# Meta tokens brought in turned by 16 element-wise transfers, output quarters 3 turned off TensorE, and the decay gates' steps moved one unit forward, in a three-layer fp32 kernel

## The chip, the cores and the metric

One NeuronCore of a Trainium2 chip runs the whole program. The metric is the device time of one execution in microseconds, the median of several runs. Lower is better.

## What is computed

A 256 x 2048 activation `x` goes through three layers, all in fp32. Cut to what matters here:

```
# layer 1: 16 heads, stick-breaking attention
q, k, v, g = split(rms_norm(x) @ w_in_a, 4);  o = attention(q, k, v)
x = x + rms_norm((o * silu(g)) @ w_out_a);    x = x + (p0 @ w_pp0) * sigmoid(x @ w_pg0)
# layer 2: 16 heads, latent attention
cq, g = split(rms_norm(x) @ w_in_b);          o = mla(rms_norm(cq) @ w_uq, k, v)
x = x + rms_norm((o * silu(g)) @ w_out_b);    x = x + (p1 @ w_pp1) * sigmoid(x @ w_pg1)
# layer 3: 16 meta tokens (16 x 2048) are put ahead of the 256 rows
h = concat([meta_tokens, x])
q, k, v, r, glr, pu = split(rmsnorm(h) @ w_in)
logg = log_sigmoid(glr @ gate_w2 + gate_b) / 16      # the decay gates
... gated linear attention in chunks of 64 (sums of logg), pooling, w_out, MLP, final norm
```

Every weight is read once from HBM. Each fp32 product is made of three products of rounded parts (high x high, high x low, low x high).

## The kernel before, in words

**Weights.** All weight matrices come in units of 128 partitions x 1024 fp32 (512 KB), numbered through the whole program by `plan()`. SyncE (SP) loads them in order into a ring of four `raw` slots (`load`, L405), one as soon as VectorE (DVE) has made the low part of the unit four before it (`lo_done`). ScalarE (ACT) makes the high part `whi` (L1155) once TensorE (PE) has used the unit four before; DVE makes the low part `wlo` (L1751); PE multiplies. A unit is 12 matmuls of 128 x 512 in most stages (L538 to L540 in `unit`) and 24 matmuls of 272 columns in the stages `k2`, `v2`, `pu` (L978 to L980 in `columns`). A chunk of a stage is eight units (four in `k2` and the like). ACT's and DVE's loops (`along`) take, for step uu of a chunk, first the split of the unit three ahead and then the "hooks" written for that step; PE's loops run the hooks of a step ahead of its matmuls. So the order of the work on each engine is written out by hand.

**Turned operands.** PE needs activations with the channel on the partitions. There are two ways. In the first, PE transposes a batch of four 128 x 128 blocks into PSUM (`batch`, L550; `turn` and `turns` call it for a tensor's eighth f), and ACT (`hi_batch`, L1193) and DVE (`lo_batch`, L1788) split it. In the second, for quarters listed in `MOVED`, nothing runs on PE: DVE transposes 32 x 32 blocks straight into place in `mov` (`blocks_turned`, L1810, four instructions a band of 32 partitions). For quarters also listed in `FLIPPED`, DVE first makes two big block transposes into `stg` (`flipped`, L1799), then ACT copies two of the four bands (`bands_moved`, L1207, four each) and DVE makes the other two itself. Then ACT splits the high part (`hi_moved`, L1216, L1220) and DVE the low part (`lo_moved`, L1823, L1827). PE's wait for a quarter is in `operands`. `mov` holds one quarter at a time, so one quarter's band copies wait for the low part of the quarter before.

The gated attention output, `ogA` in layer 1 and `ogB` in layer 2, is the operand of the stages `out_a` and `out_b`. Before: `ogA` quarter 2 (eighths 4 and 5) goes by DVE; quarter 3 (eighths 6 and 7) and all of `ogB` go through PE. PE makes eighths 6 and 7 at unit 4 of the first chunk of `out_a` and `out_b` (`OG_LATE`) and needs them at unit 6. DVE writes the last quarter of the gated output (`gated`, L1985) just ahead of that chunk.

**Meta tokens.** One DMA (L468) brings them as 16 rows into `metax`. At unit 6 of the last chunk of `gate1` PE turns them (`turn_meta`, 16 transposes of 16 x 128 into one PSUM bank, L550). DVE multiplies them by the norm gain (L1999) into `scaledM`; ACT takes the squares of `metax` (L1367, four), then copies the high part `lhi` (L1370); DVE makes the low part `llo` (L2002). PE waits for that low part between the last chunk of `gate1` and the stage `q2`.

**Decay gates.** In the first chunk of `k2` PE makes the gate logits ahead of unit 2 (`gate_logits`, L915 and L916). Before them come: `glrT` (DVE L2243, step 0), the high part `glrS` (ACT L1561, step 1), `gw2lo` (DVE L2248, step 1) and the low part of `glrS` (DVE L2251, step 1). Then ACT takes |.|, exp and log (L1568, L1573, L1578) in steps 2 and 3 and in step 0 of the second chunk, DVE the gates (L2259, step 1 of the second chunk), and PE sums them ahead of the second chunk's unit 3 (`sums_from_start`, L923).

Of the kernel before, what the change touches and what calls it, by code (L numbers as in the profile page):

```python
# [21 lines left out]
P = 128  # L22
# [29 lines left out]

LAST = {4: [6, 7]}
BLK = 32
FLIPPED = [("x1", 3), ("x3", 3), ("x5", 3)]
MOVED = [(name, c) for name, cs in (("ogA", [2]), ("x1", [3]), ("x2", [0, 1, 2]), ("x3", [3]), ("x4", [0, 1, 2]), ("x5", [0, 1, 2, 3])) for c in cs]
X1_LATE = {1: [4, 5]}
OG_EARLY, OG_LATE = {6: [0, 1]}, {"ogA": {0: [2, 3], 4: [6, 7]}, "ogB": {0: [2, 3], 2: [4, 5], 4: [6, 7]}}
MIXED_EARLY = {7: [0, 1]}

UNIT = 1024
# [41 lines left out]
def join(*hooks):  # L103

    return {u: [f for h in hooks for f in h.get(u, [])] for u in sorted({u for h in hooks for u in h})}
# [40 lines left out]
def build(nc, w, const, out):  # L146
# [3 lines left out]
    with ctx:  # L150
# [142 lines left out]
        def sem(name):  # L293
            if name not in sems:
                sems[name] = ctx.enter_context(nc.semaphore(name))
            return sems[name]
# [8 lines left out]


        NORMS = ("pre0", "post0", "pre1", "kvl", "ql", "post1", "norm1", "norm2")
        order = [("gcol", 1), ("x0", 8), ("p", 2), ("norms", 1), ("ogA", [0, 1, 2, 3, 6, 7]), ("x1", 6), ("x2", [6, 7]), ("ckv", 2), ("kr", 1),
                 ("cq", 2), ("ogB", [0, 1, 2, 3, 4, 5, 6, 7]), ("x3", 6), ("meta", 1),
                 ("x4", [6, 7]), ("rsb", 1), ("qdec", 2), ("kend", 2),  # L310
                 ("vT", 4), ("kvM", 1), ("mixed", 4)]
        whole = ("gcol", "norms", "kr", "rsb", "qdec", "kend", "vT", "kvM")
# [35 lines left out]
        def gate_chunk_at(j):  # L348

            return S["attb"].c0 + min(2 * j + 2, SLOTS - 1) + j  # L350
# [47 lines left out]
        def _(sp):  # L398
# [8 lines left out]
            def stage(name, lo=0, hi=None):  # L407
                s = S[name]
                for j in range(lo, s.chunks if hi is None else hi):
                    for uu in range(s.units):  # L410
                        load(s, j, uu)
# [49 lines left out]
            stage("out_b", 0, 1)  # L461
            sp.wait_ge(sem("attB_o"), HEADS // 2)
            sp.dma_start(gains[:, :], w["norm_post"][1:2, :].to_broadcast((P, D))).then_inc(sem("post_in1"), 16)
            stage("out_b", 1)
            stage("ple1")
            stage("gate1", 0, 1)
            sp.wait_ge(evac_dve, S["out_b"].c0 + 4)
            sp.dma_start(metax[0:META, :], w["meta_tokens_2"]).then_inc(sem("meta_in"), 16)  # L468
            latents = w["w_in_2"][0, :, V0 + 2 * GLA_H * DV:V0 + 2 * GLA_H * DV + GRANK].rearrange("(k p) n -> p k n", p=P)
            for j in (1, 2):  # L470
                stage("gate1", j, j + 1)
                half = slice((j - 1) * (KT // 2), j * (KT // 2))
                sp.dma_start(graw[:, half, :], latents[:, half, :]).then_inc(sem("latents_in"), 16)
            stage("gate1", 3)
# [24 lines left out]
        def _(pe):  # L499
# [236 lines left out]
                    hooks = join(hooks, {6: [lambda: pe.wait_ge(sem("attA_o"), HEADS // 2)]}, turns("ogA", OG_EARLY))  # L736
                product(S["g"], j, mhi, mlo, hooks=hooks)

            def turn_meta():
                pe.wait_ge(sem("meta_in"), 16)  # L740
                batch([(metax[0:META, k * P:(k + 1) * P], META, k * META) for k in range(KT)])

            def post(layer, y, x1, x2):

                ab = "ab"[layer]
                def gates_out():
                    pe.wait_ge(evac_act, gate_chunk_at(3) + 1)
                late = turns(y, OG_LATE[y])
                for hook in late.pop(0):
                    hook()  # L750
                for j in range(4):
                    product(S[f"out_{ab}"], j, bhi, blo, need=y if j == 0 else None, free=gates_out if layer and j == 0 else None, hooks=late if j == 0 else {})
                for j in range(4):
                    product(S[f"ple{layer}"], j, phi[:, layer], plo[:, layer])
                    if j % 2:
                        for f in (j - 1, j):
                            turn(x1, f)
                for j in range(4):
                    hooks = {} if j else turns(x1, X1_LATE)
                    if layer and j == 3:  # L760
                        hooks = join(hooks, {6: [turn_meta]})
                    product(S[f"gate{layer}"], j, *((ahi, alo) if layer else (bhi, blo)), need=x1 if j == 0 else None, hooks=hooks)

            post(0, "ogA", "x1", "x2")
# [126 lines left out]
                    mm = pe.matmul(tp[n % 2][:, META + t * P:META + (t + 1) * P], ones, diag[:, t, :], start=True, stop=True)  # L891
                mm.then_inc(tp_full, 1)

            pe.wait_ge(tp_done, BATCH["meta", 0][0] + 1)
            def latents():

                pe.wait_ge(tp_done, BATCH["x4", 7][0] + 1)
# [83 lines left out]
                    mm.then_inc(unit_used, 1)  # L981
            product(S["q2"], 0, x4hi, x4lo, need="x4", hooks=join(turns("x4", LAST), {7: [turn_rs]}))
            latents()
            columns("k2", 0, {2: [gate_logits]})
            columns("k2", 1, {3: [sums_from_start]})
            columns("v2", 0, {2: [sums_to_end]})
            columns("v2", 1, {1: [lambda f=f: turn_decayed_queries(f) for f in range(2)], 3: [lambda t=t: turn_keys(t) for t in range(TT)]})
# [150 lines left out]
        def _(act):  # L1138
# [221 lines left out]
            def meta_in():  # L1360

                act.wait_ge(sem("meta_in"), 16)
                for i in range(4):
                    n = sq[0]
                    sq[0] += 1
                    act.wait_ge(sem("squares"), n - 1)
                    act.activation(xb[n % 2][0:META, 0:CH], metax[0:META, i * CH:(i + 1) * CH], ACT.Square,  # L1367
                                   accum_out=ssqM[0:META, i:i + 1]).then_inc(sem("squares"), 1)
                act.wait_ge(sem("meta_scaled"), 1)
                act.activation(lhi[:, :, 0:META], scaledM[:, :, :], ACT.Copy).then_inc(tp_hi, 1)  # L1370
                act.wait_ge(sem("latents_in"), 32)
                act.activation(gwT[:, :, 0:GRANK], graw[:, :, :], ACT.Copy).then_inc(sem("latents_hi"), 1)

# [224 lines left out]
            def columns(name, j, dst, hooks={}):  # L1598
# [2 lines left out]
                along(s, j, hooks)  # L1601
                ended(s, j)
                act.activation(dst, acc[(s.c0 + j) % 2][0][:, 0:LEN], ACT.Copy).then_inc(evac_act, 1)
            columns("k2", 0, kT[:, 0, :], {0: [gate_hi], 1: [latents_hi], 2: [gate_abs], 3: [gate_exp]})
            columns("k2", 1, kT[:, 2, :], {0: [gate_log], 3: [exps_from_start]})
            for j, hooks in enumerate(({2: [exps_to_end]}, {}, {}, {})):
                columns("v2", j, vT[:, 2 * j, :], hooks)

# [129 lines left out]
        def _(dve):  # L1738
# [249 lines left out]
            for j in range(4):  # L1988
                along(s, j, ahead=softplus_of(3 + j), hooks=join(attention_of(3 + j), join(los("ogA", bhi, blo, None, OG_EARLY),
                                                                             {2 * q + 1: [lambda q=q: blocks_turned("ogA", 2, q)] for q in range(P // BLK)}) if j == 3 else {}))  # L1990
                gated(s.c0 + j, (s.c0 + j) % 2, j, sem("attA_o"), 2 * (j + 1))

            rsM = rs[0:META, 7, 0:1]

            def meta_in():

                n, k = BATCH["meta", 0]
                dve.wait_ge(tp_full, n + 1)
                dve.tensor_tensor(scaledM[:, :, :], tp[n % 2][:, 0:KT * META].rearrange("p (k m) -> p k m", m=META),  # L1999
                                  gcol[:, GC["norm1"]:GC["norm1"] + KT][:, :, None].to_broadcast((P, KT, META)), ALU.mult).then_inc(sem("meta_scaled"), 1)  # L2000
                dve.wait_ge(tp_hi, k + 1)
                dve.tensor_tensor(llo[:, :, 0:META], scaledM[:, :, :], lhi[:, :, 0:META].bitcast(F32), ALU.subtract).then_inc(tp_done, 1)  # L2002
                dve.wait_ge(sem("latents_hi"), 1)
                dve.tensor_tensor(gwT[:, :, GRANK:], graw[:, :, :], gwT[:, :, 0:GRANK].bitcast(F32), ALU.subtract).then_inc(sem("latents_lo"), 1)
                sq[0] += 4
                dve.wait_ge(sem("squares"), sq[0] + 6)
                dve.tensor_reduce(ssumM[0:META, :], ssqM[0:META, :], AX, ALU.add).then_inc(sem("metan_ssum"), 1)
# [192 lines left out]
            for c in range(SLOTS):  # L2200
                more = c + 1 < SLOTS
                scores_out(c)
                for k, (query, uu) in enumerate(slot_units(c)):
                    split_to(u + 4)
                    u += 1
                    if query and uu == 1:
                        dve.wait_ge(unit_used, u)
                        queries_out(c + 1, (*acc[0], tp[0]))
                    if more and k == 3:
                        roped_queries(c + 1)  # L2210
                    if more and k == 4:
# [90 lines left out]

            def values_turned(h):
                turned_out("vT", h, vC[:, :, h * DV:(h + 1) * DV])
            columns("k2", 0, kT[:, 0, :], kT[:, 1, :], sem("kT"), {0: [latents_out], 1: [latents_split]})
            columns("k2", 1, kT[:, 2, :], kT[:, 3, :], sem("kT"), {1: [log_gates]})
            for j, hooks in enumerate(({1: [keys_from_start], 3: [keys_to_end]},
                                       {1: [lambda f=f: decayed_queries_out(f) for f in range(2)],
                                        3: [lambda t=t: turned_out("kend", t, kend[:, t, :]) for t in range(TT)]},
# [234 lines left out]
```

## Time and profile before

| | |
|---|---|
| median of 3 runs (lowest to highest) | 2059.88 us (2059.24 to 2059.95) |
| the profiled execution's own time | 2059.53 us |
| its span in the profile | 2057.7 us |
| PE busy | 2046.2 us (99%) |
| DVE busy | 1315.2 us (64%) |
| ACT busy | 1103.1 us (54%) |
| DMA traffic | 375.49 MB, q1 at 60.0% of 16 engines |

A busy time is the time in which an engine had a compute instruction in flight. PE's matmuls are pipelined: the start of one to the start of the next (0.23 us for 512 columns) is what one costs, while its own duration is shown as 0.39 us. So what a group of instructions costs PE is read from starts. The profiled time is 0.35 us under the median, and 1.8 us of it lie outside the span.

### The profile page before, as it was taken

What the parts mean: (1) busy time and instruction counts of PE and PEld (TensorE: products, weight loads), DVE (VectorE), ACT (ScalarE), POOL (GpSimd) and SP (SyncE); (2) the same over time, 40 slices, a digit from 0 to 9 for tenths busy, and PEclk for the clock granted to TensorE, in tenths of its full rate; (3) what the DMA queues carried; (4) which work ended last, traced back from release to release, by engine and by line L of the source; (5) the groups of instructions that cost most, each with busy time, mean ns of one, the idle gap of its engine ahead of it and who ended that gap; (6) DMA issues with size and microseconds to landing.
All of it is one profiled execution on the core that took longest, in us unless ns stands there. A gap on an engine that the chain in (4) does not pass through costs nothing.

```text
span 2057.7 us, 27144 instructions
## 1 busy us (share of the span) xinstructions
PE 2046.2 (99%) x10712; PEld 1755.5 (85%) x10712; DVE 1315.2 (64%) x1722; ACT 1103.1 (54%) x1581; POOL 6.1 (0%) x12
## 2 busy tenths in 40 slices
PE   9999999999999999999999999999999999999998
PEld 8888888888898888888889988888888888888886
DVE  6555556757877777658955567976556556555554
ACT  6444566646566787546664355565335434434444
POOL 0000000000000000000000000000000000000000
PEclk9999999999999999999999999999999999999999
DMA  8666655665656555565645446666666666666664
GB/s 278 186 186 192 174 154 155 188 191 173 201 173 191 169 143 164 182 194 184 195 148 155 137 140 224 194 192 186 195 195 185 194 195 185 193 193 189 191 195 144
DMA packets 211165, 375.49 MB, mean 182 GB/s; under 512 B 13875, under 2 KB 48917, under 8 KB 210518
## 3 DMA queue, kind: packets, MB, share of 16 engines
q1 hardware_dynamic: 211046, 373.85, 60.0%
q8 instruction: 81, 1.33, 0.3%
q14 instruction: 38, 0.31, 0.1%
HBM read 371.71 MB, written 2.10 MB: 182 GB/s over the span
## 4 chain that ended last, share of the span: by engine, by line
PE 98%; ACT 1%; DVE 0%; DMA 0%; issue 0%; SPq 0%; ACTq 0%; DVEq 0%
PE acc L538 19%; PE acc L540 19%; PE acc L539 19%; PE acc L1094 6%; PE acc L644 3%; PE tp L1094 3%; PE xb L1094 3%; PE acc L1097 3%; PE acc L978 2%; PE acc L980 2%; PE acc L979 2%; PE tp L644 1%; PE xb L644 1%; PE acc L647 1%; PE xb L1097 1%; PE tp L1097 1%
## 5 line engine op out<-in xcount | busy, mean ns | idle before, releaser
L1751 DVE TENSOR_TENSOR wlo<-raw,whi 128x1024 fp32r<-128x1024 f32 x633 | 771.9, 1224 | 591.8 <-ACT whi L1155 589.8
L1155 ACT ACTIVATE whi<-raw 128x1024 fp32r<-128x1024 f32 x633 | 668.3, 1059 | 741.0 <-PE acc L540 430.5
L538 PE MATMUL acc<-whi,both 128*128 128x512 f32 (+1 forms) x976 | 375.8, 385 | 0.0
L540 PE MATMUL acc<-whi,both 128*128 128x512 f32 (+1 forms) x976 | 374.0, 383 | 0.0
L539 PE MATMUL acc<-wlo,both 128*128 128x512 f32 (+1 forms) x976 | 373.8, 383 | 0.0
L540 PEld LDWEIGHTS acc<-whi,both 128*128 128x128 f32 x976 | 183.2, 188 | 36.1
L538 PEld LDWEIGHTS acc<-whi,both 128*128 128x128 f32 x976 | 183.3, 188 | 34.7
L539 PEld LDWEIGHTS acc<-wlo,both 128*128 128x128 f32 x976 | 183.3, 188 | 34.0
L1094 PE MATMUL acc<-bT,whi 128*128 128x512 f32 x512 | 160.7, 395 | 0.0
L538 PE MATMUL acc<-whi,bhi 128*128 128x512 f32 x384 | 150.0, 391 | 0.0
L540 PE MATMUL acc<-whi,blo 128*128 128x512 f32 x384 | 149.5, 389 | 0.0
L539 PE MATMUL acc<-wlo,bhi 128*128 128x512 f32 x384 | 149.4, 389 | 0.0
L1097 PEld LDWEIGHTS acc<-bT,wlo 128*128 128x128 f32 x512 | 96.2, 188 | 22.7
L538 PE MATMUL acc<-whi,aT 128*128 128x512 f32 x256 | 101.4, 396 | 0.0
L1097 PE MATMUL acc<-bT,wlo 128*128 128x256 f32 x512 | 100.6, 278 | 0.0
L540 PE MATMUL acc<-whi,aT 128*128 128x512 f32 x256 | 99.9, 390 | 0.0
L539 PE MATMUL acc<-wlo,aT 128*128 128x512 f32 x256 | 99.7, 389 | 0.0
L978 PE MATMUL acc<-lhi,whi 128*128 128x272 f32 x320 | 93.4, 292 | 0.0
L980 PE MATMUL acc<-lhi,wlo 128*128 128x272 f32 x320 | 92.2, 288 | 0.0
L979 PE MATMUL acc<-llo,whi 128*128 128x272 f32 x320 | 91.5, 286 | 0.0
L540 PEld LDWEIGHTS acc<-whi,blo 128*128 128x128 f32 x384 | 72.1, 188 | 15.1
L539 PEld LDWEIGHTS acc<-wlo,bhi 128*128 128x128 f32 x384 | 72.1, 188 | 14.8
(417 smaller groups left out, 3191.2 us busy)
## 6 DMA issues: line engine op xcount, KB each, us to landing
raw<-in_mlp_w SPq DMA_DIRECT2D x256, 512.0 KB, 4.3
raw<-in_w_in_a SPq DMA_DIRECT2D x128, 512.0 KB, 3.8
raw<-in_w_ple_gate SPq DMA_DIRECT2D x64, 512.0 KB, 4.3
raw<-in_w_in SPq DMA_DIRECT2D x64, 512.0 KB, 3.8
raw<-in_w_in_b SPq DMA_DIRECT2D x40, 512.0 KB, 3.9
raw<-in_w_out_a SPq DMA_DIRECT2D x32, 512.0 KB, 4.2
raw<-in_w_out_b SPq DMA_DIRECT2D x32, 512.0 KB, 4.3
raw<-in_w_out SPq DMA_DIRECT2D x32, 512.0 KB, 4.5
```

What stands on the lines that cost most here:

```text
L538: pe.matmul(o, hi[:, kt, tok], whi[:, slot, wc], start=start, stop=False)
L539: pe.matmul(o, hi[:, kt, tok], wlo[:, slot, wc], start=False, stop=False)
L540: mm = pe.matmul(o, lo[:, kt, tok], whi[:, slot, wc], start=False, stop=stop)
L644: pe.matmul(tiles[q % 2][ct][:, :], whi[:, slot, wc[ct]], aT[:, kt, :, :].rearrange("p i t -> p (i t)"), start=first and k == 0, stop=False)
L647: mm = pe.matmul(tiles[q % 2][ct][:, 0:SEQ], wlo[:, slot, wc[ct]], aT[:, kt, 0, :], start=False, stop=end)
L978: pe.matmul(o, whi[:, slot, wc], lhi[:, kt, :], start=first and k == 0, stop=False)
L979: pe.matmul(o, whi[:, slot, wc], llo[:, kt, :], start=False, stop=False)
L980: mm = pe.matmul(o, wlo[:, slot, wc], lhi[:, kt, :], start=False, stop=last and k == s.kt - 1)
L1094: pe.matmul(banks[ct][:, :], whi[:, slot, wc[ct]], bT[:, kt, :, :].rearrange("p i t -> p (i t)"), start=first and k == 0, stop=False)
L1097: mm = pe.matmul(banks[ct][:, 0:SEQ], wlo[:, slot, wc[ct]], x5hi[:, kt, :], start=False, stop=end)
L1155: act.activation(whi[:, u % RING, 0:n], raw[:, u % RING, 0:n], ACT.Copy).then_inc(hi_done, 1)
L1751: dve.tensor_tensor(wlo[:, u % RING, 0:n], raw[:, u % RING, 0:n], whi[:, u % RING, 0:n].bitcast(F32), ALU.subtract).then_inc(lo_done, 1)
```

## The change

Three edits. (1) `ogA` and `ogB` quarter 3 join `FLIPPED` and `MOVED` (so do the eighths 6 and 7 leave `OG_LATE`): DVE flips the quarter right behind the last `gated`, ACT and DVE move its bands, split it in step 4 of the first chunk. (2) Meta tokens are loaded a second time, turned, by 16 DMAs of 128 x 16 single elements into `scaledM`, one behind every third weight unit from the second chunk of `out_b` to the third of `gate1`; `turn_meta` leaves PE, and DVE multiplies `scaledM` in place. The plain load of `metax` stays, for the squares. (3) In `k2` the gates' steps move: ACT's high part to step 0, |.| to 1, exp to 2, log to 3; DVE's split to step 0 and its gates to step 0 of the second chunk; PE's logits to unit 1. PE's sums stay where they are.

```diff
-FLIPPED = [("x1", 3), ("x3", 3), ("x5", 3)]
-MOVED = [... ("ogA", [2]), ("x1", [3]), ("x2", [0, 1, 2]), ("x3", [3]), ...]
+FLIPPED = [("ogA", 3), ("x1", 3), ("ogB", 3), ("x3", 3), ("x5", 3)]
+MOVED = [... ("ogA", [2, 3]), ("x1", [3]), ("x2", [0, 1, 2]), ("ogB", [3]), ("x3", [3]), ...]
-OG_EARLY, OG_LATE = {6: [0, 1]}, {"ogA": {0: [2, 3], 4: [6, 7]}, "ogB": {0: [2, 3], 2: [4, 5], 4: [6, 7]}}
+OG_EARLY, OG_LATE = {6: [0, 1]}, {"ogA": {0: [2, 3]}, "ogB": {0: [2, 3], 2: [4, 5]}}
 # SP
-            stage("out_b", 1)
-            stage("ple1")
-            stage("gate1", 0, 1)
+            def with_meta(name, lo, hi, first):
+                s = S[name]
+                for j in range(lo, hi):
+                    for uu in range(s.units):
+                        load(s, j, uu)
+                        m = first + (j - lo) * s.units + uu
+                        if m % 3 == 2 and m // 3 < KT:
+                            k = m // 3
+                            sp.dma_start(scaledM[:, k, :], w["meta_tokens_2"][:, k * P:(k + 1) * P].rearrange("m p -> p m"), allow_slow_non_contiguous=True).then_inc(sem("meta_turned"), 16)
+            with_meta("out_b", 1, NCH, 0)
+            with_meta("ple1", 0, NCH, 24)
+            with_meta("gate1", 0, 1, 28)
...
-                stage("gate1", j, j + 1)
+                with_meta("gate1", j, j + 1, 28 + 8 * j)
 # PE
-                    if layer and j == 3:
-                        hooks = join(hooks, {6: [turn_meta]})
-            pe.wait_ge(tp_done, BATCH["meta", 0][0] + 1)
+            pe.wait_ge(sem("meta_lo"), 1)
-            columns("k2", 0, {2: [gate_logits]})
+            columns("k2", 0, {1: [gate_logits]})
 # ACT
-            columns("k2", 0, kT[:, 0, :], {0: [gate_hi], 1: [latents_hi], 2: [gate_abs], 3: [gate_exp]})
-            columns("k2", 1, kT[:, 2, :], {0: [gate_log], 3: [exps_from_start]})
+            columns("k2", 0, kT[:, 0, :], {0: [gate_hi, latents_hi], 1: [gate_abs], 2: [gate_exp], 3: [gate_log]})
+            columns("k2", 1, kT[:, 2, :], {3: [exps_from_start]})
 # DVE, behind the last gated() of layer 1 (and the same for layer 2)
+            dve.wait_ge(evac_dve, s.c0 + 4)
+            flipped(nat, 3, 1)
-                dve.wait_ge(tp_full, n + 1)
-                dve.tensor_tensor(scaledM[:, :, :], tp[n % 2][:, 0:KT * META]..., gcol[...], ALU.mult)
+                dve.wait_ge(sem("meta_turned"), 16 * KT)
+                dve.tensor_tensor(scaledM[:, :, :], scaledM[:, :, :], gcol[...], ALU.mult)
-            columns("k2", 0, kT[:, 0, :], kT[:, 1, :], sem("kT"), {0: [latents_out], 1: [latents_split]})
-            columns("k2", 1, kT[:, 2, :], kT[:, 3, :], sem("kT"), {1: [log_gates]})
+            columns("k2", 0, kT[:, 0, :], kT[:, 1, :], sem("kT"), {0: [latents_out, latents_split]})
+            columns("k2", 1, kT[:, 2, :], kT[:, 3, :], sem("kT"), {0: [log_gates]})
```

## Rows read from the trace of the kernel before

**Rows 1.** The page: the chain that ended last, share of the span by engine.
```profile
PE 98%; ACT 1%; DVE 0%; DMA 0%; issue 0%; SPq 0%; ACTq 0%; DVEq 0%
```

**Rows 2.** Waits of PE: who waited for whom, us in total, times, longest.
```profile
PE tp L915 <- DVE glrS L2251: 0.7, 1, 0.7
```

**Rows 3.** Timeline of PE, first chunk of out_a: start us, us, instruction.
```profile
408.89 0.39 PE L540 MATMUL acc<-whi,blo 128*128 128x512 f32 x1
...
410.23 0.40 PE L539 MATMUL acc<-wlo,bhi 128*128 128x512 f32 x1
...
415.45 0.39 PE L538 MATMUL acc<-whi,bhi 128*128 128x512 f32 x1
```

**Rows 4.** Timeline of DVE around the start of out_a.
```profile
399.03 1.23 DVE L1985 TENSOR_TENSOR nat<-nat,stg 128x1024 f32<-128x1024 f32 x1
400.17 1.22 DVE L1751 TENSOR_TENSOR wlo<-raw,whi 128x1024 fp32r<-128x1024 f32 x1
401.31 1.28 DVE L1788 TENSOR_TENSOR blo<-tp,bhi 128x512 fp32r<-128x512 f32 x2
...
403.64 1.22 DVE L1823 TENSOR_TENSOR blo<-mov,bhi 128x1024 fp32r<-128x1024 f32 x1
```

**Rows 5.** Timeline of DVE at the start of out_b, then PE at its unit 4.
```profile
838.22 1.23 DVE L1985 TENSOR_TENSOR nat<-nat,stg 128x1024 f32<-128x1024 f32 x1
...
849.71 1.03 PE L550 MATMUL tp<-tab,nat 128*128 128x128 f32 x8
```

**Rows 6.** Timeline of DVE, then ACT, where x1's flipped quarter is moved.
```profile
501.58 1.30 DVE L1799 STREAM_TRANSPOSE stg<-x 128x512 f32<-128x512 f32 x2
...
508.19 1.79 DVE L1810 STREAM_TRANSPOSE mov<-x 32x256 f32<-32x256 f32 x4
...
502.91 1.70 ACT L1207 ACTIVATE mov<-stg 32x256 f32<-32x256 f32 x4 [1.29 <-DVE stg L1799]
```

**Rows 7.** Timeline of PE: end of gate1, start of q2.
```profile
1021.76 0.39 PE L540 MATMUL acc<-whi,both 128*128 128x512 f32 x1
...
1023.51 0.40 PE L539 MATMUL acc<-wlo,both 128*128 128x512 f32 x1
...
1028.75 0.40 PE L538 MATMUL acc<-whi,lhi 128*128 128x512 f32 x1
...
1037.05 0.40 PE L538 MATMUL acc<-whi,lhi 128*128 128x512 f32 x1
```

**Rows 8.** Timeline of ACT, then DVE, in the same stretch.
```profile
1027.27 0.40 ACT L1370 ACTIVATE lhi<-scaledM 128x256 fp32r<-128x256 f32 x1
...
1027.70 0.42 DVE L2002 TENSOR_TENSOR llo<-scaledM,lhi 128x256 fp32r<-128x256 f32 x1 [0.72 <-ACT lhi L1370]
...
1035.36 4.62 DVE L1751 TENSOR_TENSOR wlo<-raw,whi 128x1024 fp32r<-128x1024 f32 x4
```

**Rows 9.** Timeline of PE, then DVE, at the gates in k2.
```profile
1062.48 0.29 PE L980 MATMUL acc<-lhi,wlo 128*128 128x272 f32 x1
1063.50 0.48 PE L915 MATMUL tp<-gw2hi,glrS 65*128 65x512 f32 x1 [0.73 <-DVE glrS L2251]
...
1079.85 0.29 PE L980 MATMUL acc<-lhi,wlo 128*128 128x272 f32 x1
1080.54 2.05 PE L923 MATMUL tp<-tab,logg 128*128 128x128 f32 x16 [0.40 <-DVE loggM L2259]
...
1062.81 0.43 DVE L2251 TENSOR_TENSOR glrS<-glrT,glrS 32x272 fp32r<-32x272 f32 x1
```

**Rows 10.** DMA in 970.0 to 970.5 us: packets, then queue, MB, share.
```profile
DMA packets 575, 0.08 MB, mean 164 GB/s; under 512 B 552, under 2 KB 552, under 8 KB 575
...
q1 hardware_dynamic: 575, 0.08, 111.6%
```

**Rows 11.** DMA in 969.0 to 969.5 us: the queue, packets, MB, share.
```profile
q1 hardware_dynamic: 60, 0.12, 75.3%
```

**Rows 12.** Second chunk of gate1: engines' busy us; last, PE clock, DMA share, GB/s.
```profile
962.00:984.00 22.00, 22.00 (x99) 18.23 (x98) 20.12 (x31) 12.34 (x19) 0.00 (x0) 1.00 0.65 207
```

More of the change, by code:

```diff
@@ L54 @@
 BLK = 32
-FLIPPED = [("x1", 3), ("x3", 3), ("x5", 3)]
-MOVED = [(name, c) for name, cs in (("ogA", [2]), ("x1", [3]), ("x2", [0, 1, 2]), ("x3", [3]), ("x4", [0, 1, 2]), ("x5", [0, 1, 2, 3])) for c in cs]
+FLIPPED = [("ogA", 3), ("x1", 3), ("ogB", 3), ("x3", 3), ("x5", 3)]
+MOVED = [(name, c) for name, cs in (("ogA", [2, 3]), ("x1", [3]), ("x2", [0, 1, 2]), ("ogB", [3]), ("x3", [3]), ("x4", [0, 1, 2]), ("x5", [0, 1, 2, 3])) for c in cs]
 X1_LATE = {1: [4, 5]}
-OG_EARLY, OG_LATE = {6: [0, 1]}, {"ogA": {0: [2, 3], 4: [6, 7]}, "ogB": {0: [2, 3], 2: [4, 5], 4: [6, 7]}}
+OG_EARLY, OG_LATE = {6: [0, 1]}, {"ogA": {0: [2, 3]}, "ogB": {0: [2, 3], 2: [4, 5]}}
 MIXED_EARLY = {7: [0, 1]}
@@ L307, in build @@
         NORMS = ("pre0", "post0", "pre1", "kvl", "ql", "post1", "norm1", "norm2")
-        order = [("gcol", 1), ("x0", 8), ("p", 2), ("norms", 1), ("ogA", [0, 1, 2, 3, 6, 7]), ("x1", 6), ("x2", [6, 7]), ("ckv", 2), ("kr", 1),
-                 ("cq", 2), ("ogB", [0, 1, 2, 3, 4, 5, 6, 7]), ("x3", 6), ("meta", 1),
+        order = [("gcol", 1), ("x0", 8), ("p", 2), ("norms", 1), ("ogA", [0, 1, 2, 3]), ("x1", 6), ("x2", [6, 7]), ("ckv", 2), ("kr", 1),
+                 ("cq", 2), ("ogB", [0, 1, 2, 3, 4, 5]), ("x3", 6),
                  ("x4", [6, 7]), ("rsb", 1), ("qdec", 2), ("kend", 2),
@@ L737, in _ @@
                 product(S["g"], j, mhi, mlo, hooks=hooks)
-            def turn_meta():
-                pe.wait_ge(sem("meta_in"), 16)
-                batch([(metax[0:META, k * P:(k + 1) * P], META, k * META) for k in range(KT)])
             def post(layer, y, x1, x2):
@@ L1369, in meta_in @@
                 act.wait_ge(sem("meta_scaled"), 1)
-                act.activation(lhi[:, :, 0:META], scaledM[:, :, :], ACT.Copy).then_inc(tp_hi, 1)
+                act.activation(lhi[:, :, 0:META], scaledM[:, :, :], ACT.Copy).then_inc(sem("meta_hi"), 1)
                 act.wait_ge(sem("latents_in"), 32)
@@ L1991, in _ @@
                 gated(s.c0 + j, (s.c0 + j) % 2, j, sem("attA_o"), 2 * (j + 1))
+            dve.wait_ge(evac_dve, s.c0 + 4)
+            flipped(nat, 3, 1)
             rsM = rs[0:META, 7, 0:1]
             def meta_in():
-                n, k = BATCH["meta", 0]
-                dve.wait_ge(tp_full, n + 1)
-                dve.tensor_tensor(scaledM[:, :, :], tp[n % 2][:, 0:KT * META].rearrange("p (k m) -> p k m", m=META),
+                dve.wait_ge(sem("meta_turned"), 16 * KT)
+                dve.tensor_tensor(scaledM[:, :, :], scaledM[:, :, :],
                                   gcol[:, GC["norm1"]:GC["norm1"] + KT][:, :, None].to_broadcast((P, KT, META)), ALU.mult).then_inc(sem("meta_scaled"), 1)
-                dve.wait_ge(tp_hi, k + 1)
-                dve.tensor_tensor(llo[:, :, 0:META], scaledM[:, :, :], lhi[:, :, 0:META].bitcast(F32), ALU.subtract).then_inc(tp_done, 1)
+                dve.wait_ge(sem("meta_hi"), 1)
+                dve.tensor_tensor(llo[:, :, 0:META], scaledM[:, :, :], lhi[:, :, 0:META].bitcast(F32), ALU.subtract).then_inc(sem("meta_lo"), 1)
                 dve.wait_ge(sem("latents_hi"), 1)
@@ L2218, in _ @@
                     gated(gate_chunk_at(c // 2), 0, c // 2, sem("attB_o"), c + 1)
+            dve.wait_ge(evac_dve, gate_chunk_at(3) + 1)
+            flipped(nat, 3, 1)
             post(1, "ogB", "x3", "x4", GC["norm1"], "norm1")
```

## The prediction

> **What bounds the kernel now.** I read the chain that ended last first: 98% of the span is PE's own work [rows 1]. So the time is the sum of PE's instructions plus PE's few waits. Second, the list of PE's waits. It has five rows, the longest 1.1 us at the very start; the largest that the change touches is the gate logits' wait for DVE [rows 2], and the sums' wait of 0.40 us is in the timeline [rows 9]. No weight unit is waited for, so raw DMA arrival bounds nothing yet. Third, the timelines of PE, DVE and ACT at the four places that the change touches: an item taken from PE pays in full only if the item that PE then meets is ready. Last, the DMA, since the change adds transfers to SP's only queue: its engines were busy 65% of a chunk of `gate1` [rows 12].
>
> What a piece of work costs PE is the gap between the starts around it less the steady pitch of 0.2277 us.
>
> **Part 1: output quarters off PE.** Removed at unit 4 of `out_a`: eight transposes. From L540 at 408.89 to L539 at 410.23 are 1.34 us, two pitches are 0.455, so they cost 0.885 us [rows 3]. `out_b` has the same pattern. Gross 1.77 us.
> What comes instead must be ready when PE enters unit 6. For `out_a` that is 415.45 - 0.885 = 414.57. DVE, in order: the gating ends at 399.03 + 1.23 = 400.26 [rows 4]; the flip waits for it, then takes 1.30 [rows 6], to about 401.6. Then L1751 at a pitch of 1.14 (400.17 to 401.31) and the two L1788 at about 1.19 [rows 4]: 402.7, 403.9. Step 1: L1751, L1823 at 1.14 each: 406.2. Step 2: L1751 and four band transposes (1.82 with their start) [rows 6]: 409.2. Step 3, the same: 412.1. Step 4: L1751, 413.3, then the low split, to be begun at 413.4 and done, at 1.22, at 414.6. ACT does not set this: its first bands wait for the low split of quarter 2 at 406.3, take 1.70 each [rows 6], and with two weight splits between them end at about 410.8, before DVE's. Its high split needs DVE's last band (412.2) and is done by 413.3.
> From the end of a DVE result to PE's start were 0.05 us for `loggM` and 0.26 for `glrS` (62.81 + 0.43 to 63.50) [rows 9]. So PE can start unit 6 between 414.65 and 414.86, against 414.57: a new wait of 0.1 to 0.3 us, I take 0.2. Net for `ogA`: 0.69. Queued behind DVE's flip are only weight splits three units ahead, which have 8 us.
> For `out_b` there is no quarter 2 in the way. The gating ends at 839.45 [rows 5], the flip at 840.8, steps 0 to 3 hold four L1751, two pairs of L1788 and two sets of bands (4.56 + 2.38 + 3.64): 851.4; the last L1751 and the low split: 853.8. PE enters unit 6 at 849.71 + 2 x 2.73 = 855.17 [rows 5]. Spare 1.3 us, so the full 0.885 comes. Eighths 4 and 5 slip by 1.3 us and still come 1.3 ahead of unit 4. Bounds: `ogA` 0 to 0.885, `ogB` 0.5 to 0.885. Part 1: **1.57 us**.
>
> **Part 2: meta tokens.** Removed from PE at unit 6: L540 at 1021.76 to L539 at 1023.51 are 1.75, less 0.455: 1.30 us [rows 7]. But PE then waits ahead of `q2` for `llo`, which was done at 1027.70 + 0.42 = 1028.12 [rows 8]. The chain behind it (ACT: weight split, high split of x4, four squares, `lhi`; then DVE) starts at PE's end of unit 5 and holds nothing that the change takes away; the PSUM read that DVE is spared had already landed. PE would arrive at 1028.75 - 1.30 = 1027.45 and go on at 1028.17 to 1028.38: gain 0.37 to 0.58. A second gate stands behind: `wlo` of `q2`'s unit 3 is the first of four at 1035.36, done by 1036.6 [rows 8], PE used it at 1037.05 [rows 7], and it hangs on ACT's same chain. That lets 0.2 to 0.4 through. I take **0.3 us** of 1.30; bounds 0 and 0.4.
>
> **Part 3: the 16 transfers.** Each moves 128 x 16 single elements: 2048 pieces, 128 for each of 16 DMA engines. The trace has no 4-byte pieces. The nearest row is the load of the gate columns, pieces of 64 B: in half a microsecond 111.6% of 16 engines, 8.9 us, went to 552 small and 23 large pieces [rows 10]; large ones take 0.753 x 0.5 x 16 / 60 = 0.100 us [rows 11]; so (8.9 - 2.3) / 552 = 12 ns a piece. Upper bound: a 4-byte piece as dear as a large one, 100 ns; lower bound: nothing. I take 12 ns, the nearest row: 128 x 12 = 1.5 us of all engines for each transfer. They stand behind every third unit, over 48 units or 131 us, of which 35% are free [rows 12], 46 us; 16 x 1.5 = 25 us fit. A single one delays a weight unit by 1.5 us; a unit is asked for some 8 us ahead of ACT's use and landed in about 4.3 (page), and ACT and DVE are up to three units (8 us) ahead of PE. SP's issue took 0.47 us for the gate columns, and SP mostly waits. Cost **0**. If the cover goes: per piece t ns, 16 x 0.128 t us less 46 us less some 12 us of lead; the point is near 28 ns, and each 10 ns beyond cost 20 us. At 100 ns it is 147 us.
> The Trainium skill speaks against this edit ("DMA: Bandwidth & Descriptors", section "Rules for kernel authors"): a last dimension that isn't contiguous becomes one descriptor for each element, and a plain DMA with a rearranged pattern is 19 times slower than the hardware transpose. Estimate from that page: if the 128 KB went at 19 times the cost at the weights' rate here (some 300 GB/s when busy, 0.43 us), they would take 8 us in all, and still be hidden; by the row of 64-byte pieces it is 25 us. Either leaves the sum as it is.
>
> **Part 4: gates a step ahead.** The logits: L980 at 1062.48 to L915 at 1063.50 is 1.02, the pitch there 0.125 us, so 0.89 lost [rows 9]. The last input, the low part of `glrS`, now hangs on `glrT` (done 1057.2) plus ACT 0.42 and DVE 0.43 with a 0.68 us split beside: ready by 1058.5. PE meets it a unit (3.0 us) sooner than before, at 1059.6: no wait, 0.89 won. The sums: 1079.85 to 1080.54 is 0.69, less 0.125: 0.57 lost [rows 9]. The log now ends in the first chunk's step 3, at about 1072.3; DVE's gates follow the chunk's evacuation and one weight split, 1074.8 to 1076.8. PE comes at about 1079.1: no wait, 0.57 won. ACT's and DVE's weight splits behind the moved steps are 1 to 3 us later than PE frees them, against three units of lead. Part 4: **1.45 us**; bounds 0.9 and 1.5.
>
> **Sum.** 1.57 + 0.3 + 0 + 1.45 = 3.3 us, from the profiled 2059.53 to 2056.2; the median of the runs lies 0.35 higher, so 2059.88 - 3.3 = **2056.6 us**. About 0.2% (4.1 us) is what a measurement can tell from no change: faster means under 2055.8, slower over 2064.0. So the forecast is "no change that can be told", by a small real gain.
>
> **Rivals.**
> (a) Slower: the element-wise DMAs cost more than 28 ns a piece. All 2048 pieces of one transfer read 4 B out of 16 short stretches of 512 B, which 64-byte pieces did not do; this speaks for it. Against: 64-byte pieces already were far below the large ones and took 12 ns. At 36 ns a piece (three times the row): 16 x 4.6 - 58 = 16 us, 2056.6 + 16 = 2073. Decides from 28 ns on. Chance 0.16.
> (b) Faster by over 0.2%: every removed piece pays in full: 1.77 + 1.30 + 1.45 = 4.5 us, 2055.4. For it: PE is 98% of the chain. Against: the chain behind `llo` ends 0.7 us after PE would come. It decides from 4.1 us on; also without the meta part's full gain, if cold starts saved elsewhere add 0.8. Chance 0.13.
> (c) Less comes: DVE, 20.1 us busy of 22 in `gate1` [rows 12], is late behind delayed weights or flips, and `ogA`'s wait is 0.9, not 0.2. Gain 1.5 to 2, 2058.1. Chance 0.18.
> (d) The change doesn't do what it says, the gates' wait only moves: PE at unit 1 waits for ACT's `glrS`. Gain 1.9, 2058.0. Against: ACT sat idle 4.8 us there. Chance 0.03.
> Forecast: 0.50.
>
> **How the numbers follow.** Forecast, (c) and (d) are within 0.2%, 0.71; with the ends of (b) that fall short, and the small overruns of (a) that are under 4 us, taken as they stand: faster 0.13, same 0.70, slower 0.17. Range: down to 2055.4, all of (b)'s price; up past (c) to 2061.5, a start of (a), which leaves out most of (a)'s 0.16. The likeliest case's own range is 2056.0 to 2057.6.
>
> **What would show it.** L550's groups at unit 4 of `out_a` and `out_b` and the 16 x 16 one in `gate1` gone. PE's waits: none at L915 and L923; new ones of 0.1 to 0.3 us at `out_a`'s unit 6 for `blo` (L1823's place) and of about 0.8 us at `q2`'s first matmul for `llo`. The DMA share in `out_b` and `gate1` up from 0.65 to about 0.8, with 32768 more small pieces, and no ACT split waiting long for `raw`. I am wrong if PE's waits name `wlo` in `out_b` to `gate1` (then (a)), if the wait ahead of `q2` is missing (then (b)), or if `out_a`'s unit 6 starts on time.

## Result and profile after

The changed kernel takes 2124.87 us, median of 4 runs (2122.51 to 2126.32), against 2059.56 us for the kernel before: ratio 1.0315, 95% interval [1.0303, 1.0327]. It is 65 us slower where 3.3 us less were forecast. Its profiled execution is the one of 2126.32 us, span 2124.5 us.

Two lines of its page follow: the engines' busy time, and the chain that ended last, where [rows 1] had PE at 98%.

```profile
PE 2068.4 (97%) x10680; PEld 1765.9 (83%) x10680; DVE 1324.1 (62%) x1740; ACT 1110.0 (52%) x1595; POOL 6.1 (0%) x12
```

```profile
PE 87%; DMA 9%; DVE 2%; SPq 1%; ACT 0%; issue 0%; ACTq 0%
```

DMA now holds 9% of the chain. PE's waits (us in total, times, longest), of which [rows 2] has gone:

```profile
PE acc L547 <- DVE wlo L1754: 38.0, 13, 5.8
PE acc L547 <- ACT pp L1415: 2.6, 1, 2.6
PE acc L547 <- DVE llo L2006: 2.3, 1, 2.3
PE tp L559 <- DVE both L1791: 2.1, 1, 2.1
```

`wlo` in `out_b` to `gate1` is what the prediction named as the sign that it is wrong. DVE is not the cause: it waits for ACT's `whi`, and the waits of ACT say what ACT stood for:

```profile
ACT whi L1158 <- DMA raw<-in_w_out_b: 54.1, 17, 10.5
ACT whi L1158 <- DMA raw<-in_w_ple_gate: 50.6, 17, 10.6
```

In the kernel before, ACT waited for neither. So the weights come late. The list of DMA issues (number, KB, us to landing) has `out_b`'s weight units at 10.3 us, while `out_a`'s, with no turned transfer among them, stayed at 4.3, and a turned one of 8 KB at 15.9:

```profile
raw<-in_w_out_a SPq DMA_DIRECT2D x32, 512.0 KB, 4.3
raw<-in_w_out_b SPq DMA_DIRECT2D x32, 512.0 KB, 10.3
...
scaledM<-in_meta_tokens SPq DMA_DIRECT2D x16, 8.0 KB, 15.9
```

SP's timeline in `out_b` (start, us, instruction) shows the period: one turned transfer, three units, and the next one 12.1 to 13.7 us later, where PE takes 8.2 us for three units. Most of the time in `load` (L405) is SP waiting for a free buffer.

```profile
862.31 0.77 SPq L472 DMA_DIRECT2D scaledM<-in_meta_tokens  x1
863.12 12.89 SPq L405 DMA_DIRECT2D raw<-in_w_out_b  x3
876.05 0.47 SPq L472 DMA_DIRECT2D scaledM<-in_meta_tokens  x1
876.56 11.59 SPq L405 DMA_DIRECT2D raw<-in_w_out_b  x3
888.19 1.92 SPq L472 DMA_DIRECT2D scaledM<-in_meta_tokens  x1
```

The lists of the 16 turned transfers, of this kernel and of the one cut by token (below), which is free of the fault, give their first and last issue; the third line is the landing here:

```profile
L472 SPq DMA_DIRECT2D scaledM<-in_meta_tokens x16: 472/710/1922, 850.1 to 1038.2; - x16
...
L472 SPq DMA_DIRECT2D scaledM<-in_meta_tokens x16: 465/472/1025, 849.6 to 976.4; - x16
...
DMA to landing us min/median/max: 14.2/15.9/17.4
```

The 15 periods take 188.1 us against 126.8, 12.5 each against 8.5: 61 of the 70 us between the two spans. The DMA of a single microsecond within such a stretch (869 to 870: packets, then queue, packets, MB, share of 16 engines) shows what a turned transfer does:

```profile
DMA packets 279, 0.01 MB, mean 11 GB/s; under 512 B 274, under 2 KB 274, under 8 KB 279
...
q1 hardware_dynamic: 279, 0.01, 15.6%
```

274 small pieces and 5 large ones go in it, and the engines count as busy 16% of the time. In [rows 10] 552 small pieces went in half that time beside 23 large ones. The pieces are few and their engines idle: they are held by something that the busy share does not show. That is why the DMA share, which I wanted at about 0.8, fell; windows of a stretch of `out_b`, then of `gate1` (columns as in [rows 12]):

```profile
861.00:900.00 39.00, 30.71 (x122) 24.23 (x121) 12.24 (x12) 11.68 (x17) 0.00 (x0) 0.91 0.45 122
...
1020.00:1040.00 20.00, 14.22 (x55) 11.29 (x53) 9.43 (x16) 4.28 (x7) 0.00 (x0) 0.83 0.36 94
```

The granted clock is under 1 as well. After a wait of 4.76 us PE goes on at a pitch of 0.43 us instead of 0.2277, and the clock granted from 882.6 to 886 is 0.50, the lower of the two levels (1.2 of 2.4 GHz):

```profile
882.67 0.79 PE L547 MATMUL acc<-whi,bhi 128*128 128x512 f32 x1 [4.76 <-DVE wlo L1754]
883.27 0.63 PE L548 MATMUL acc<-wlo,bhi 128*128 128x512 f32 x1
883.69 0.63 PE L549 MATMUL acc<-whi,blo 128*128 128x512 f32 x1
...
887.96 0.51 PE L547 MATMUL acc<-whi,bhi 128*128 128x512 f32 x1
888.31 0.40 PE L548 MATMUL acc<-wlo,bhi 128*128 128x512 f32 x1
```

Against the version by token (PE busy 2043.9 us, PE's waits 2.6 us, span 2054.5) the 70.0 us are 45.4 us more of PE waiting (48.0 in all) and 24.5 us more of PE busy with as many instructions. This splits PE's time; it does not make the slower matmuls a second cause. The DMA's own time already gives the period: 7.7 us for a turned transfer (first look, below) and 4.9 us for three weight units (60% of 8.2 us, the DMA share before) are 12.6 us, and 12.5 were measured. In `out_b` each turned transfer is issued, 10.8 to 13.7 us after the one before it, when that one has not landed (14.2 us at least). And the period with the slow matmuls above in it (876.05 to 888.19) took 12.1 us, the one before it, at full clock, 13.7. So the slow matmuls seem to fill time in which PE would else have waited; that they lengthened a period is not shown.

### The profile page after: what moved, and what is told of

Read it like the earlier page. It is cut to its first block, busy times and chain, and to the rows that moved or that the text cites. A ratio compares the mean times of both kernels' runs of the same rounds, so it can differ in the third digit from the quotient of the medians.

```text
span 2124.5 us, 27125 instructions
## 1 busy us (share of the span) xinstructions
PE 2068.4 (97%) x10680; PEld 1765.9 (83%) x10680; DVE 1324.1 (62%) x1740; ACT 1110.0 (52%) x1595; POOL 6.1 (0%) x12
## 2 busy tenths in 40 slices
DMA packets 244189, 375.62 MB, mean 177 GB/s; under 512 B 46899, under 2 KB 81941, under 8 KB 243542
## 4 chain that ended last, share of the span: by engine, by line
PE 87%; DMA 9%; DVE 2%; SPq 1%; ACT 0%; issue 0%; ACTq 0%
PE acc L547 16%; PE acc L548 16%; PE acc L549 16%; PE acc L1097 6%; DMA raw<-in_w_ple_gate 4%; DMA raw<-in_w_out_b 3%; PE acc L653 3%; PE tp L1097 3%; PE xb L1097 3%; PE acc L1100 3%; PE acc L981 2%; PE acc L983 2%; PE acc L982 2%; PE tp L653 1%; PE xb L653 1%; PE acc L656 1%
## 5 line engine op out<-in xcount | busy, mean ns | idle before, releaser
L547 PE MATMUL acc<-whi,both 128*128 128x512 f32 (+1 forms) x976 | 380.5, 390 | 16.7 <-DVE wlo L1754 16.3
L549 PE MATMUL acc<-whi,both 128*128 128x512 f32 (+1 forms) x976 | 377.3, 387 | 0.0
L547 PEld LDWEIGHTS acc<-whi,both 128*128 128x128 f32 x976 | 185.7, 190 | 55.1 <-DVE wlo L1754 15.0
L549 PEld LDWEIGHTS acc<-whi,both 128*128 128x128 f32 x976 | 185.4, 190 | 37.1
L547 PEld LDWEIGHTS acc<-whi,bhi 128*128 128x128 f32 x384 | 73.6, 192 | 36.8 <-DVE wlo L1754 21.3
## 6 DMA issues: line engine op xcount, KB each, us to landing
raw<-in_w_out_b SPq DMA_DIRECT2D x32, 512.0 KB, 10.3
```

The source lines that it names most:

```text
L547: pe.matmul(o, hi[:, kt, tok], whi[:, slot, wc], start=start, stop=False)
L549: mm = pe.matmul(o, lo[:, kt, tok], whi[:, slot, wc], start=False, stop=stop)
```

## Experiments

**First look: what makes such a transfer dear.** Three theories: (1) the count, any DMA of 2048 pieces takes this long; (2) reads that meet: all 2048 pieces read 4 B out of 16 short stretches of 512 B; (3) the 4 bytes, as against 64. Single transfers of six shapes were put among the weights of the MLP stages of the kernel before, three of each, in one run:

```
"A": (probe[:, 0, :], meta[:, 0:P].rearrange("m p -> p m")),   # as the change
"B": (probe[:, :, 0], lat[:, :, 0]),                # 2048 x 4 B, each from another row
"C": (many, lat[:, :, 0:META]),                     # 2048 x 64 B
"D": (probe[:, 0, :], lat[:, 0, 0:META]),           # 128 x 64 B
"E": (probe[:, 0, 0:4], meta[0:4, 0:P].rearrange("m p -> p m")),   # 512 x 4 B
"F": (probe[0:META]..., meta[:, 0:P]),              # 16 x 512 B
```

> The kernel before, with 18 lone transfers issued from SP in the MLP stages, one behind every 12th weight unit, each into a dead buffer: six shapes, three times each. A: 2048 pieces of 4 B from the meta tokens, as the change has it (16 stretches of 512 B are read). B: 2048 pieces of 4 B, each from another row of w_in_2. C: 2048 pieces of 64 B from the same rows as B. D: 128 pieces of 64 B. E: 512 pieces of 4 B from the meta tokens. F: 16 pieces of 512 B. Theory 1 (a cost by the number of pieces, paid one after another, wherever they are read and however long they are: in the changed kernel some 200 small pieces a us flowed while the DMA engines were busy to a fifth): A, B and C each land in 12 to 16 us, E in 4 to 5, D and F in 2 to 3. Theory 2 (the reads of A meet in the same short stretches of memory): A 12 to 16 us, B and C 4 to 6, E 4 to 5. Theory 3 (pieces under 64 B are dear to write): A and B 12 to 16 us, C 5 to 6. Time: under all three within 5 us of before, since a lone one has 12 units (33 us) to be made up.

From issue to landing, us, min/median/max, for A, B, C in turn (the trace's lists for the three lines):

```profile
DMA to landing us min/median/max: 14.4/14.5/15.6
...
DMA to landing us min/median/max: 5.2/5.3/5.4
...
DMA to landing us min/median/max: 5.0/5.1/6.3
```

D took 4.2, E 5.3, F 4.0. As many 4-byte pieces from 2048 rows (B) cost what 64-byte ones cost (C): theories 1 and 3 fall. F reads the same 16 stretches whole in 4.0, so it is not the place alone but the many small reads of it. What A does to others is in the DMA strips, 40 slices of 0.45 us, of the stretch with the first A (1340 to 1358) and of the one with the first B (1378 to 1396):

```profile
DMA  2069499510000000000000000012458977999999
GB/s 105 0 59 82 105 391 414 116 1 1 1 1 1 1 1 1 1 1 1 1 1 1 1 1 1 0 5 64 146 182 228 232 214 246 355 378 391 405 401 373
```

```profile
DMA  5599694799996859987966649940977950995970
```

During A all 16 engines together move 1 GB/s for 17 slices, 7.7 us, recorded as busy under a tenth of the time, and a waiting weight unit moves nothing. 7.7 us / 128 pieces for each engine is 60 ns a piece. PE waited 2 x 2.2 us in the 26 us after the first A; the kernel as a whole took 2065.54 us against 2059.63, with 18 probes, 3 of them A.

**Second look: which reads meet.** Again 2048 pieces of 4 B each, in one run. Theory 2 is split: (2a) the step of 8 KB, or of another power of two, between rows; (2b) neighbouring elements, at whatever step.

```
"G": 16 stretches of 512 B, rows 16448 B apart (w_in_2)
"H": elements 64 B apart, over the whole 8 KB of 16 rows
"I": one row, 8 KB on end
"J": 16 stretches of 512 B, rows 32 KB apart (w_in_a)
"K": elements 16 B apart, 2 KB of each of 16 rows
```

> The kernel before, with 18 lone transfers in the MLP stages as in the first probes (there the change's own shape landed in 14.5 us, the same number of 4 B pieces from 2048 different rows in 5.3 us), all of 2048 pieces of 4 B, six sources, three times each. A: as the change, 128 neighbouring elements of each of 16 meta rows, rows 8 KB apart. G: the same from w_in_2, rows 16448 B apart. J: the same from w_in_a, rows 32 KB apart. K: elements 16 B apart in the meta rows, 2 KB of each. H: elements 64 B apart, the whole 8 KB of each row. I: one whole meta row, 8 KB in one stretch, 128 neighbours at each of 16 places 512 B apart. Theory 2a (it is the 8 KB step between rows, a power of two, that sends the reads to one place of the memory): A and J 14 us, G and I 5 to 6 us, H 14 us. Theory 2b (it is neighbouring elements, many reads within one short stretch, at whatever step): A, G, J and I about 14 us, H 5 to 6, K between. Time: within 10 us over before.

Medians: A 14.1, G 10.9, J 8.0, K 5.7, H 5.6, I 5.6 us; 2063.72 us in all against 2059.76. Neither theory holds: 2a wanted 14 for J and H and 5 to 6 for G, 2b wanted 14 for G, J and I. 512 B read in 128 pieces are slow when 16 such stretches are some KB apart, and slower at 8 KB than at 16.4 or 32 (G and J read other tensors, too); the same 128 neighbours in 16 stretches on end (I), or elements 16 B apart and more (K, H), are not. H and K write just as A does, so it is not the writes. Shown is that the map of the reads decides, both the 4 B between elements and the KB between stretches, and not their count or size. That reads "meet" is not shown: I reads its 8 KB as densely as A reads its stretches. What in the memory makes this map stays open.

**Quarters and gates alone**, the meta tokens loaded in rows and turned on TensorE as before:

```
-                sp.dma_start(scaledM[:, k, :], ...rearrange("m p -> p m"), ...)   # all 16
+            def turn_meta():
+                pe.wait_ge(sem("meta_in"), 16)
+                batch([(metax[0:META, k * P:(k + 1) * P], META, k * META) for k in range(KT)])
```

> The changed kernel with the meta tokens as before (turned on PE, no element-wise transfers): only the output quarters and the gates are changed. Theory A (the transfers alone made the kernel slower, and the other parts do what the prediction said, 1.57 + 1.45 us): 3.0 us under before, 2056.5 to 2056.9. Rival (the flips and the earlier gate steps make new waits of their own on PE): 0 to 10 us over before, with waits of PE at out_a, out_b or k2.

2056.67 us against 2059.63, ratio 0.9985 [0.9976, 0.9994]: -2.96 us, with no wait at the gates. The whole loss comes with the part taken out.

**The same 16 transfers with few pieces**, 128 of 64 B (other data):

```
-  sp.dma_start(scaledM[:, k, :], w["meta_tokens_2"][:, k * P:(k + 1) * P].rearrange("m p -> p m"), ...)
+  sp.dma_start(scaledM[:, k, :], w["w_in_2"][0, k * P:(k + 1) * P, 0:META])
```

> The changed kernel; its 16 transfers stay at their places and carry the same 8 KB each, but as 128 pieces of 64 B (other data, so the meta tokens' values are not those of the reference). Theory 1, 2 and 3 all say: the cost goes, 2056 to 2058 us. Rival (an extra DMA in SP's queue costs in itself, by its fixed latency or by SP's issue): 4 us or more for each, 2110 to 2125 us as the changed kernel.

2056.70 us, ratio 0.9986 [0.9977, 0.9996], landing in 4.3. So 16 more DMAs at these places in SP's queue cost nothing; what is in them does.

**From GpSimd's queue**, so that no weight unit stands behind a turned transfer in SP's:

```
+            for k in range(KT):
+                pool.wait_ge(lo_done, S["out_b"].u0 + 8 + 3 * k)
+                pool.dma_start(scaledM[:, k, :], ...)
```

> The changed kernel; the same 16 transfers of 2048 pieces are issued from GpSimd, which is idle there, at the same distance of three weight units. Theory 1 in the form that the pieces are made one after another on SP's own queue and hold up the weights behind them: the weights on SP's queue flow freely, 2056 to 2062 us. Theory 1 in the form of a part that all queues share, theories 2 and 3 (the engines or the memory are what is held): the weights still land late, 2080 to 2130 us.

2146.32 us (2139.92 to 2146.94), ratio 1.0411 [1.0396, 1.0427]; landing 15.0 to 23.0, and PE's first wait, as a list of waits has it:

```profile
PE acc L538 <- DVE wlo L1745: 47.3, 17, 6.5
```

It is not the order in SP's queue. The transfers hold up weight units of another queue too, and this version is 21 us worse still. Why was not followed up; its transfers are issued 3.6 to 26.2 us apart, where those from SP are 10.8 to 16.9 apart, so the queue is not all that differs.

**Cut by token.** If the map of the reads is the cause, the same 32,768 elements in 16 transfers are cheap once each transfer reads one row on end (shape I). By 2b alone they would stay dear:

```
-  sp.dma_start(scaledM[:, k, :], w["meta_tokens_2"][:, k * P:(k + 1) * P].rearrange("m p -> p m"), ...)
+  sp.dma_start(scaledM[:, :, k], w["meta_tokens_2"][k].rearrange("(k p) -> p k", p=P), ...)
```

> The changed kernel with the same 16 transfers of 2048 elements cut the other way: each brings one token (one meta row of 8 KB, contiguous in memory) for all 16 column blocks, where the change brings all 16 tokens for one block. Same places, same number and size of pieces, same result. Theory 2a (the 8 KB step): the transfers land in 5 to 6 us, the cost goes, 2056 to 2058 us. Theory 2b (neighbours): as the changed kernel, 2110 to 2130 us.

2055.93 us (2055.70 to 2056.90, 11 runs) against 2059.76: ratio 0.9982 [0.9973, 0.9991], -3.8 us. Landing:

```profile
DMA to landing us min/median/max: 4.3/5.2/6.5
```

The page's packet lines, of this kernel and of the changed one, have the same 46899 pieces under 512 B; only their grouping differs. Windows in `out_b` and `gate1`, the second the same as [rows 12]:

```profile
861.00:900.00 39.00, 39.00 (x173) 32.30 (x173) 19.70 (x19) 17.77 (x22) 0.00 (x0) 1.00 0.77 191
962.00:984.00 22.00, 22.00 (x99) 18.22 (x98) 20.52 (x31) 12.65 (x20) 0.00 (x0) 1.00 0.88 229
```

PE is never idle, at full clock. Before, the first stretch had a DMA share of 0.62 and the second 0.65 [rows 12]:

```profile
861.00:900.00 39.00, 39.00 (x173) 32.29 (x172) 20.26 (x19) 17.55 (x23) 0.00 (x0) 1.00 0.62 194
```

From the rise follows an estimate of the price of a piece: (0.77 - 0.62) x 39 x 16 engines / (4.8 transfers x 2048) is 10 ns a piece, (0.88 - 0.65) x 22 x 16 / (2.7 x 2048) is 15. This is about the price that the prediction used, 12.

**Cut finer and spread wide**: 64 transfers of 512 elements (4 tokens, shape E), one for every three units from stage `g` on, into another free buffer:

```
+  if (u - 136) % 3 == 0 and 0 <= n < 4 * KT:
+      k, m = n // 4, slice(n % 4 * 4, n % 4 * 4 + 4)
+      sp.dma_start(scaledM[:, k, m], w["meta_tokens_2"][m, k * P:(k + 1) * P].rearrange("m p -> p m"), ...)
```

> The changed kernel; the same elements in 64 transfers of 512 pieces (4 tokens x 128), one behind every third weight unit from the stage g of layer 1 to gate1, into another free buffer. The first probes had 512 such pieces landed in 4.5 to 6.2 us, 2 us over a plain one. Theory (what counts is how long one transfer holds the queue against some 8 us of lead, not the sum of 64 x 2.5 us = 160 us): the cost goes, 2056 to 2058 us. Rival (the sum is paid, as the queue has only 35 of 100 free and 3 x 2.73 us minus 4.9 us of weights leave 3.3 us): 5 to 40 us over.

2061.91 us (2059.31 to 2063.91), ratio 1.0010 [1.0001, 1.0019]: mostly hidden, but not the 2056 to 2058 of the theory. One wait of 3.4 us for `wlo` is left, and it is 5 us over the kernel with quarters and gates alone and 6 us over the cut by token. Spreading a dear transfer helps; making it cheap helps more.

**What the meta part gains.** Three kernels on one chip, 11 runs each: by token with the scale and split of the turned tokens moved to the first steps of `gate1`'s last chunk (below for DVE; ACT's high part goes to step 1); by token as it was; quarters and gates alone.

```
-  ... hooks, {6: [meta_in], 7: [meta_rs]}) if layer and j == 3 ...
+  ... {0: [meta_scale], 2: [meta_low]}, hooks, {6: [meta_in], 7: [meta_rs]}) if layer and j == 3 ...
```

> The kernel with the transfers cut by token, and the scale and the high/low split of the turned meta tokens moved from behind gate1's last unit to steps 0, 1 and 2 of its last chunk, since their transfers have landed by then. Theory of the prediction's Part 2: PE's wait ahead of q2 is for llo, the end of a chain of DVE and ACT behind gate1, so with llo ready some 15 us earlier the wait of about 0.6 us goes, and a later gate (the weight split of one of q2's first units) lets 0.2 to 0.9 us through: 0.2 to 0.9 us under the kernel cut by token. Rival: the wait only changes its name, because the same chain of ACT work holds x4's own parts, and the time is that of the kernel cut by token within 0.1 us; and if the splits crowd ACT or DVE in gate1's last chunk it is slower, with a PE wait for wlo there.

> The kernel with the 16 transfers cut by token once more, on the same chip as the next one, so that the two differ by the meta part alone. Theory (prediction, Part 2): removing the transpose of the meta tokens gives 0.3 us, at most 0.4, for PE waits for llo instead: 0.3 us under the next one. Rival: all 1.3 us come. With a wait for llo of 0.6 us in the trace, 0.4 to 0.7 would fit too.

> Quarters and gates alone, the meta tokens loaded in rows and turned on TensorE as before, on the same chip: 3.0 us under the kernel before (Part 1 and Part 4), and 0.3 us over the kernel cut by token if the meta part gains what the prediction took, 1.3 us over it if all of it comes.

2056.52, 2056.62 and 2056.59 us, all at 0.9984 [0.9975, 0.9993] of 2059.88: by time the meta part gains nothing that can be told (0.3 us were expected, 1.3 by the rival, 0.2 to 0.9 more from the early split). The timelines are sharper. PE at `q2`'s first matmul and at its unit 3, by token, then with the early split:

```profile
1027.10 0.39 PE L549 MATMUL acc<-whi,both 128*128 128x512 f32 x1
1028.07 0.51 PE L547 MATMUL acc<-whi,lhi 128*128 128x512 f32 x1 [0.58 <-DVE llo L2006]
1028.42 0.39 PE L548 MATMUL acc<-wlo,lhi 128*128 128x512 f32 x1
...
1036.24 0.39 PE L549 MATMUL acc<-whi,llo 128*128 128x512 f32 x1
1036.62 0.47 PE L547 MATMUL acc<-whi,lhi 128*128 128x512 f32 x1
1036.93 0.39 PE L548 MATMUL acc<-wlo,lhi 128*128 128x512 f32 x1
```

```profile
1034.36 0.39 PE L549 MATMUL acc<-whi,llo 128*128 128x512 f32 x1
1035.43 0.47 PE L547 MATMUL acc<-whi,lhi 128*128 128x512 f32 x1 [0.69 <-DVE wlo L1756]
1035.74 0.39 PE L548 MATMUL acc<-wlo,lhi 128*128 128x512 f32 x1
```

By token PE loses 1.32 - 0.455 = 0.865 us ahead of `q2` and 0.69 - 0.455 = 0.235 at unit 3: 1.10 in place of the 1.30 of the transposes, a gain of 0.20. With the early split the wait for `llo` is gone and the one for `wlo` of unit 3 grows to 1.38 - 0.455 = 0.925: a gain of 0.37. Two gates stand one behind the other, and the second holds what the first lets through.

## Why the prediction was wrong

The step that failed is Part 3, its price of a piece: "I take 12 ns, the nearest row", and with it its cost of 0. The runs show 60 ns for these pieces. The rest of the step then fits: put into the prediction's own formula, 16 x 0.128 x 60 - 58 = 65 us, and the transfers cost 65.3 + 3.0 = 68. (The 12 us of lead in the 58 were an estimate that no run measured.) The point of 28 ns was passed twofold. The mechanism that came is rival (a), and the sentence that spoke for it (all pieces of one transfer read 4 B out of 16 short stretches) names a property that the probes then confirmed in part: the short stretches count, but only with KB between them (I is cheap). I gave it 0.16 and priced it at three times the row, since the 64-byte pieces of [rows 10] seemed the nearest; they were near in size, but each lay in a row of its own, as B and C do. ("The trace has no 4-byte pieces" goes too far: the page of before has 13875 pieces under 512 B, and the gate columns are 2048 of them.) I had only bounds of 0 and 100 ns and no row that shared the pattern of reads; between ends that far apart, with 147 us at one of them, 0.16 was too little, and a range up to 2061.5 did not take in the upper bound as it should have. The paragraph that turns the chances into numbers also makes 0.70 of its 0.71 and 0.17 of (a)'s 0.16, for no reason that it gives.

The Trainium skill, "DMA: Bandwidth & Descriptors", section "Rules for kernel authors", warned against a plain DMA with a rearranged pattern, 19 times slower than the hardware transpose. The direction was right for the changed kernel; the 8 us that I worked out from it were not: 16 holds of 7.7 us are 123 us. For the cut by token, also element by element, the same rule has no cost that the time shows.

Another rule of the Trainium skill is near to the cause: the same page, section "Latency and other measured facts", has copies of large tiles slow down as the row pitch in HBM grows over large powers of two, and gives aliasing of memory channels as an inference. Its pitches are 512 KiB and more, far from those here, so it forecasts nothing for this case. Among these probes the order is another: stretches on end gave 5.6 us, a pitch of 8 KB 14.1, 16448 B 10.9 and 32 KB 8.0. No run here shows the mechanism.

The other parts, point by point:
- **Part 1**, 1.57 us. Held. In the kernel with quarters and gates alone, unit 4's transposes are gone in both stages, and PE enters `out_a`'s unit 6 so:

```profile
414.59 0.39 PE L540 MATMUL acc<-whi,blo 128*128 128x512 f32 x1
414.91 0.50 PE L538 MATMUL acc<-whi,bhi 128*128 128x512 f32 x1
415.25 0.39 PE L539 MATMUL acc<-wlo,bhi 128*128 128x512 f32 x1
```

0.66 - 0.455 = 0.20 us lost, the wait that the DVE walk gave as 0.1 to 0.3. `out_b` has no gap at its unit 6. Net 0.68 + 0.885.
- **Part 2**, 0.3 of 1.30 us. Held: 0.20, behind the two gates that it named, in that order.
- **Part 4**, 1.45 us. Held, a little over. The same kernel, with quarters and gates alone, at the logits, then at the sums:

```profile
1058.17 0.29 PE L980 MATMUL acc<-lhi,wlo 128*128 128x272 f32 x1
1058.30 0.40 PE L915 MATMUL tp<-gw2hi,glrS 65*128 65x512 f32 x1
...
1077.58 0.29 PE L980 MATMUL acc<-lhi,wlo 128*128 128x272 f32 x1
1077.71 1.95 PE L923 MATMUL tp<-tab,logg 128*128 128x128 f32 x16
1079.41 0.38 PE L978 MATMUL acc<-lhi,whi 128*128 128x272 f32 x1
```

Both steps of 1.02 and 0.69 us [rows 9] are 0.13, and the sums' own work on PE, which no longer follows a wait, takes 1.70 in place of 1.81 (before, 1080.54 to 1082.35): 0.89 + 0.57 + 0.11 = 1.57.
- **Sum.** 1.57 + 0.20 + 1.57 = 3.3 us, the sum forecast, and 3.3 to 3.8 was measured by token. Rivals (b), (c) and (d) did not come: the meta part did not pay in full, `ogA`'s wait stayed 0.2, and no gate is waited for.

Of the signs that the prediction named, the vanished groups and waits, `blo` at unit 6 and `llo` ahead of `q2` came as told; the DMA share of about 0.8 came only with the cut by token (0.77 and 0.88), and `wlo` from `out_b` to `gate1` was the sign of (a).

## What to carry to other kernels

Price a DMA of single elements by where its reads fall, not by their size or number: take the same elements so that one transfer reads one long stretch, or elements well apart, before giving up the turned load. When a cost has bounds far apart and no row that shares its pattern, put the whole upper end into the range, and look for a row with the same addresses, not the same size. Where a stretch becomes bound by the DMA, add up what the DMA has to do in one period (here 7.7 + 4.9 us against PE's 8.2) rather than PE's waits: the waits show only 45 of the 70 us, as PE also ran slower after them.

## What the hardware showed that was not expected

- One DMA of 2048 4-byte reads from 16 stretches of 512 B, 8 KB apart, keeps all 16 engines at 1 GB/s for 7.7 us, and weights late also when it comes from another queue than theirs; its engines are recorded as busy under a tenth of that time (16% in a microsecond with 5 large pieces). A low DMA share is then no sign of free room.
- The same number of 4-byte reads from 2048 rows, or from 8 KB on end, lands in 5.3 to 5.6 us, like 2048 pieces of 64 B (5.1). By the rise of the DMA share a piece read from 8 KB on end costs an estimated 10 to 15 ns.
- From GpSimd's queue, and at less even distances, the same transfers cost 21 us more than from SP's.
- The version cut by token takes 2055.93 us against 2059.76 before and 2124.87 after; by time it can't be told from quarters and gates alone.
